# Making the shift columns of block two's up projections at tile 4 of the output projection

## What is computed

```python
x_lat = x_lat + g1 * y_lat          # y_lat: output projection of the mixer
x_lat = x_lat + g2 * conv_ffn(rmsnorm(x_lat, norm_ffn) * (1 + sc2) + sh2, *ffn)
# context tokens likewise, in layer 0 only

def conv_ffn(h, w_up, conv_w, conv_b, w_down):
    g, u = jnp.split(h @ w_up, 2, axis=-1)
    g = dwconv(g, conv_w) + conv_b
    return (jax.nn.silu(g) * u) @ w_down
```

## Time and profile before

| | |
|---|---|
| runs | 3284.90, 3291.71, 3295.43 us |
| median | 3291.71 us |
| span of the profiled execution | 3283.7 us |
| mean granted TensorE clock | 0.963 |
| PE busy | 3050.2 us (93%) |
| DVE busy | 1899.8 us (58%) |
| ACT busy | 1119.9 us (34%) |

### The profile page before, as it was taken

How to read it: one execution, slowest core, us unless ns; L and a number is a source line. 1 busy time by engine, 2 the same in 40 slices (tenths; PEclk the granted TensorE clock), 3 DMA queues, 4 the chain that set the end, 5 groups by cost and what they waited for, 6 DMA issues and landing times. The chain is left out here.

```text
span 3283.7 us, 39921 instructions
## 1 busy us (share of the span) xinstructions
PE 3050.2 (93%) x16274; PEld 2693.9 (82%) x16274; DVE 1899.8 (58%) x2841; ACT 1119.9 (34%) x1658; POOL 90.5 (3%) x74
## 2 busy tenths in 40 slices
PE   7988999999879999999967789999999889999998
PEld 5767888887768888899946389999999867689997
DVE  5754775856555878765546664542553355456464
ACT  4443422235344222433335123221222245333232
POOL 0031000000130000000000000000000000000000
PEclk9998999999999999999978889999999989999999
DMA  3100554521103556412100121121122110123222
GB/s 127 50 28 20 174 176 143 191 86 52 46 7 109 194 173 193 140 58 103 58 7 1 56 82 53 65 66 57 65 64 65 69 56 8 61 85 98 91 93 87
DMA packets 73136, 275.78 MB, mean 84 GB/s; under 512 B 7835, under 2 KB 11419, under 8 KB 71804
## 3 DMA queue, kind: packets, MB, share of 16 engines
q1 hardware_dynamic: 72956, 273.25, 25.1%
HBM read 264.83 MB, written 8.39 MB: 83 GB/s over the span
## 5 line engine op out<-in xcount | busy, mean ns | idle before, releaser
L122 PE MATMUL banks<-normed_hi,weights_hi 128*128 128x384 f32 (+2 forms) x2672 | 887.9, 338 | 11.5 <-DVE normed_lo L1030 11.5
L123 PE MATMUL banks<-normed_lo,weights_hi 128*128 128x384 f32 (+2 forms) x2672 | 885.1, 337 | 0.0
L104 ACT ACTIVATE weights_hi<-weights_raw 128x1024 fp32r<-128x1024 f32 (+3 forms) x365 | 395.6, 1084 | 1244.0 <-PE banks L125 1218.7
L125 PE MATMUL banks<-normed_hi,weights_lo 128*128 128x384 f32 (+2 forms) x2672 | 742.9, 338 | 0.0
L110 DVE TENSOR_TENSOR weights_lo<-weights_raw,weights_hi 128x1024 fp32r<-128x1024 f32 (+3 forms) x365 | 459.9, 1260 | 138.0 <-ACT weights_hi L104 134.5
L122 PEld LDWEIGHTS banks<-normed_hi,weights_hi 128*128 128x128 f32 x2672 | 504.1, 189 | 39.8 <-DVE normed_lo L1030 12.2
L123 PEld LDWEIGHTS banks<-normed_lo,weights_hi 128*128 128x128 f32 x2672 | 506.3, 189 | 27.3
L125 PEld LDWEIGHTS banks<-normed_hi,weights_lo 128*128 128x128 f32 x2672 | 473.4, 190 | 27.4
L123 PE MATMUL banks<-hidden_lo,weights_hi 128*128 128x512 f32 (+1 forms) x880 | 323.0, 367 | 0.0
L122 PE MATMUL banks<-hidden_hi,weights_hi 128*128 128x512 f32 (+1 forms) x880 | 323.0, 367 | 0.0
L125 PE MATMUL banks<-hidden_hi,weights_lo 128*128 128x512 f32 (+1 forms) x880 | 294.7, 367 | 0.0
(11 more groups left out here) (424 smaller groups left out, 4248.1 us busy)
## 6 DMA issues: line engine op xcount, KB each, us to landing
weights_raw<-in_w_up SPq DMA_DIRECT2D x176, 512.0 KB, 3.4
ada_tiles<-in_ada SPq DMA_DIRECT2D x96, 512.0 KB, 3.5
weights_raw<-in_w_down SPq DMA_DIRECT2D x64, 704.0 KB, 4.0
weights_raw<-in_w_in SPq DMA_DIRECT2D x67, 512.0 KB, 3.4
weights_raw<-in_w_out SPq DMA_DIRECT2D x32, 512.0 KB, 3.4
x_kept<-x SPq DMA_DIRECT2D x2, 3072.0 KB, 10.5
x<-x_kept SPq DMA_DIRECT2D x1, 3072.0 KB, 10.0
weights_raw<-in_mla_down SPq DMA_DIRECT2D x6, 512.0 KB, 3.4
```

The costliest lines, as they stand in the source:

```text
L104: act.activation(self.hi[:, n % 2, 0:w], self.raw[:, n % 2, 0:w], ACT.Copy).then_inc(self.high_ready, 1)
L122: pe.matmul(out, self.hi[:, s, m], xh, start=k == 0, stop=False)
L123: pe.matmul(out, self.hi[:, s, m], xl, start=False, stop=False)
L125: mm = pe.matmul(out, self.lo[:, s, m], xh, start=False, stop=k == kt - 1)
```

## The change

In both layers of block two the `Shifts` object is made before the `Residual` and given to it, so that ACT's and DVE's instructions are issued at tile 4 of the output projection. In the list of stages `Shifts` becomes `ShiftsThere`, PE's wait alone.

```diff
-        mixed = Residual(Z, KT, mixed_pairs, X, SEGS, vec(0, 2, BOTH["v"]), H=H, squares=True, kept=kept)
         up_shifts, down_shifts = Shifts(Z, H, shift(0, 3)), Shifts(Z, H2, shift(1, 0))
+        mixed = Residual(Z, KT, mixed_pairs, X, SEGS, vec(0, 2, BOTH["v"]), H=H, squares=True, kept=kept,
+                         shifts=up_shifts)
...
-        Z.run(mixed, up_shifts, *ffn, Keep(Z, X, kept, lambda sp: ffn[-1].done(sp, KT - 1)),
+        Z.run(mixed, ShiftsThere(up_shifts), *ffn, Keep(Z, X, kept, lambda sp: ffn[-1].done(sp, KT - 1)),
...
-        mixed = Residual(Z, KT, form_of(latent).operand(Hm), X, latent, vec(1, 2, [0]), H=H, squares=True, kept=kept)
+        up_shifts = Shifts(Z, H, shift(1, 3))
+        mixed = Residual(Z, KT, form_of(latent).operand(Hm), X, latent, vec(1, 2, [0]), H=H, squares=True, kept=kept,
+                         shifts=up_shifts)
...
-        Z.run(mixed, Shifts(Z, H, shift(1, 3)), *ffn,
+        Z.run(mixed, ShiftsThere(up_shifts), *ffn,
```

## The result

| | before | after |
|---|---|---|
| executions | 6 | 6 |
| lowest, highest | 3281.19, 3295.43 us | 3264.00, 3267.05 us |
| median | 3287.6 us | 3265.69 us |
| ratio, 95% interval | | 0.9935 (0.9921 to 0.9950) |
| span of the profiled execution | 3283.7 us | 3265.2 us |

By medians the changed kernel is 21.9 us faster. Either the two places gave more than was worked out, or the 16.0 us were taken from the wrong number. The traces tell which.

The account below looks back on a forecast made before the run. PE was taken as the bound, held at two places by line 1030 late in DVE's queue. 8.91 + 7.07 = 15.98 us off the median 3291.7 gave 3275.7 us, range 3267 to 3285.

Parts of the forecast that it names:

- the two places: Up projections of block two, A over 768 tokens and B over 512: 8.91 and 7.07 us less, 15.98 in all.
- What bounds the kernel, and which step holds PE: PE bounds the kernel, busy 3050.2 of 3283.7 us; line 1030, last in DVE's queue, holds it at both up projections.
- The gap terms: PE's idle time between output projection and up projection of block two goes: 6.57 us at A, 5.24 at B.
- The clock terms: Without idle time PE's clock does not fall, so up tile 0 is shorter by 2.34 us at A, 1.83 at B.
- What becomes late next: In up tile 0 with PE starting at once, no input is late; thinnest margin 0.45 us, product 7 at B.
- Passed on to the end: Everything behind both places hangs on PE's column sums, so an earlier start of 8.91 us reaches the end in full.
- Nothing for tile 4: The instructions added in the output projection's tile 4 cost nothing; without cover 0.37 us at each place, 0.7 in all.
- Sum: Savings at both up projections, 8.91 + 7.07 = 15.98 us, bring the profiled span from 3283.7 to 3267.7 us.
- The step that failed: Whole kernel: the 8.0 us between profiled span and median of the runs shown was kept, giving 3291.7 - 16.0 = 3275.7 us.
- rival 1: The clock dips all the same at A or B, costing 1.83 to 2.34 us each: 3277.5 to 3279.9 us; chance 0.10.
- rival 2: PE's first product at both places hangs on the whole last input tile, gaining only 0.95 and 0.68 us: 3290.1; chance 0.07.
- rival 3: Slower: beyond 570 us of unbroken work from the output projection on, PE's clock falls, 3301.6 us or above; chance 0.03.

Follow-up runs that it names:

- filler kernel: Kernel before with its late Shifts steps, PE's idle time at both places filled with 50 and 40 unread matmuls; median 3277.2 against 3283.0 us, ratio 0.9981.
- only B: Kernel before with shift columns moved to tile 4 only for the up projection over 512 tokens; median 3277.5 us, ratio to before 0.9984.

## Why the prediction was wrong, and where it was right

*What bounds the kernel, and which step holds PE.* Right: line 1030 gone from DVE's tail, PE waits for nothing at either place.

*The gap terms, 6.57 and 5.24 us.* Right. The filler kernel leaves exactly them (6.56 and 5.24), and with the step at tile 7 they shrink to the forecast 4.64 and 3.97.

*The clock terms, 2.34 and 1.83 us.* Right in kind: without idle time the clock stays at 1.00 and tile 0 takes 8.60 and 5.80 us. As a constant they were taken too firmly. In traces whose gap is the same, tile 0 at B took 7.31 to 8.17 us, and at A 10.81 to 10.85 or, in "only B", 10.10. The Trainium skill (TensorE: Matmul & The Clock Gate, Part 1) states that the number of slow matmuls varies with when the work starts. The traces agree, with 0.7 us of variation at A and 0.9 at B. That the two places differ from each other, which the prediction took for agreement, says little on it: their gaps differ too.

*What becomes late next.* Right: nothing, and the thinnest cover is product 7 at B, forecast 0.45 us and measured as 0.4.

*Passed on to the end.* Right: from place A's column sums to the first matmul of the following mixer's projection (line 122, at 2643.39 in before and 2630.40 in after) it is 635.8 us in both, from B's to the last column sums 368.7.

*Nothing for tile 4.* Right as far as place A shows it: from the first matmul of the output projection to its last row it takes 69.0 us in before and in after.

*Sum.* 8.91 + 7.07 = 15.98 forecast, 8.91 + 7.04 = 15.95 in the traces, 17.1 (15.3 to 18.7) by means over 140 executions.

*The step that failed* is the one behind the sum: "I keep the 8.0 and predict 3291.7 - 16.0". The 8.0 us between the profiled span and the median of three were taken for something that lies around the span and would come with every execution. They don't. Most executions measured later lie 1.8 to 2.0 us above their own span, the farthest 3.9. The three times shown were one in the middle and two in the high groups; the median of 115 executions is 3283.6, 8.1 us lower. From there the sum gives 3267.6, and from the profiled execution itself, 3283.7 + 1.9 - 16.0, it is 3269.6; the measured median is 3265.7. So of the 10.0 us by which the point was missed, 6.1 are the offset. 2.5 are what the two spans differ by beyond the two places: 4.2 us in untouched stages, less what was given back. The last 1.4 us are the draw: the profiled execution of after, 3267.05, was the highest of its six.

*The range* failed with it: its lower end, 3267, was set 9 us below a point that was itself 10 us too high. The lowest of the three runs, 3284.9, less 16.0 is 3268.9, and a lower end had to allow for executions under the lowest of three. That all six executions of after fell between 3264.0 and 3267.1, where 7 of all 25 lie above 3270, is the luck of the draw; but the median of the 25, 3266.2, lies below the range as well, by 0.8 us.

*The rivals.* No dip of the clock followed the column sums at A or B in the trace of after (rival 1). The wait did not change its name (rival 2): the step at tile 7 shows PE starting under the last tile's low part. Unbroken work did not bring the clock down (rival 3): it is 1.00 from 1925 to 2560, over 635 us without a pause. What rival 1 rests on, that the clock is low while PE counts as busy, turned out larger than priced in another stage, 9 us for the filter matmuls in one trace; the prediction had looked at such stages only for the one example in the earlier trace rows.

## What to carry to other kernels

A small step behind a loop costs what stands ahead of it in its engine's queue, not its own length: 0.37 us of work at each of two places held PE for 11.8 us in all, and the idle time cost another 4 through the clock. Where the next stage waits tile by tile, a step that depends on no tile belongs well before the last one. And when three times of one program spread over 10 us, don't carry the distance between their median and one profiled span over as a constant; look for groups, and let the range start from the lowest time, not from the median.

## What the runs showed of the hardware

The granted clock can be at 0.50 while PE has no idle time: over 24 matmuls on 64 rows in one execution (19.7 us instead of 10.5), and behind 20 one-column matmuls in every trace of before (1416 to 1418 in the earlier trace rows), while in the traces of after it stays at 1.00 there. Executions of one program differ in it: of 109 executions of the kernel before, those with a mean granted clock of 0.959 to 0.962 have spans of 3284.1 us and more, and those with 0.963 to 0.965 have 3276.6 to 3283.4. What decides it in an execution stayed open.

Idle time of PE within warm work costs more than itself. Behind gaps of 6.6 us tile 0 took 1.6 to 2.4 us longer than without a gap, behind 5.2 us 1.6 to 2.5, behind 4.6 and 4.0 us 1.6 each; with the gaps filled it was 0.1 us.
